# A ninth slot for the experts' weights, and 37 small loads moved from GpSimd to ScalarE and SyncE

## The reference, cut to what matters

```python
for i in range(DEPTH):                       # two layers
    u = x @ w_in                             # conv_w_in or moba_w_in
    y = concat([mix(u), memory_attention(q_mem, mem_k, mem_v)]) @ w_o[i]
    x = layer_norm(ALPHA * x + y, ln1_g[i], ln1_b[i])
    # router: 4 groups of 8 experts, top 2 in the best group
    for g in range(4):                       # 8 experts each
        h = silu(x @ w_gate[g]) * (x @ w_up[g])
        out += (h * combine) @ w_down[g]
    x = layer_norm(ALPHA * x + out, ln2_g[i], ln2_b[i])
```

## Time and profile before

| | us |
|---|---|
| median of three executions | 2206.97 |
| the profiled execution's own time | 2208.19 |
| its span, first to last instruction | 2206.3 |
| TensorE busy | 2084.1 (94%) |
| VectorE busy | 1128.3 (51%) |
| ScalarE busy | 773.3 (35%) |
| GpSimd busy | 62.8 (3%) |

### The profile page before, as it was taken

How to read it: one execution, slowest core, us unless ns; L and a number is a source line. 1 busy time by engine, 2 the same in 40 slices (tenths; PEclk the granted TensorE clock), 3 DMA queues, 4 the chain that set the end, 5 groups by cost and what they waited for, 6 DMA issues and landing times.

```text
span 2206.3 us, 29568 instructions
## 1 busy us (share of the span) xinstructions
PE 2084.1 (94%) x12352; PEld 1470.8 (67%) x12352; DVE 1128.3 (51%) x1967; ACT 773.3 (35%) x1468; POOL 62.8 (3%) x96
## 2 busy tenths in 40 slices
PE   8989999999979899999999799999999999999998
PEld 7974433333358644333344588999888889999887
DVE  5964332222256543222222667567674676667665
ACT  4751111011035411101110355644654465544552
POOL 3000000000000000000000000011000000010000
PEclk9999999999989999999999899999999999999999
DMA  8628999999974389999999653454554724554552
GB/s 270 217 91 359 429 427 427 427 427 427 425 298 177 131 358 427 427 427 428 427 427 425 233 196 101 148 180 161 191 175 169 246 78 140 173 191 163 191 187 80
DMA packets 130251, 600.25 MB, mean 272 GB/s; under 512 B 6029, under 2 KB 26641, under 8 KB 103745
## 3 DMA queue, kind: packets, MB, share of 16 engines
q1 hardware_dynamic: 125808, 590.37, 67.8%
q10 hardware_dynamic: 3072, 6.74, 0.8%
q0 software_dynamic: 1232, 1.19, 0.4%
HBM read 597.22 MB, written 1.05 MB: 271 GB/s over the span
## 4 chain that ended last, share of the span: by engine, by line
PE 76%; DMA 16%; DVE 5%; ACT 2%; issue 1%; SPq 0%; DVEq 0%; ACTq 0%
PE ps L1609 12%; DMA ring<-in_w_up 10%; PE ps L470 7%; PE ps L1653 7%; PE ps L456 6%; PE ps L457 6%; PE ps L458 6%; DMA rx<-in_w_up 5%; PE ps L469 3%; PE ps L498 2%; PE ps L499 2%; PE ps L500 2%; PE ps L583 2%; PE ps L978 2%; PE ps L1538 1%; PE ps L3042 1%
## 5 line engine op out<-in xcount | busy, mean ns | idle before, releaser
L432 DVE TENSOR_TENSOR CL<-ring,CH 128x1024 fp32r<-128x1024 f32 x284 | 333.6, 1214 | 198.3 <-ACT CH L427 196.9
L1609 PE MATMUL ps<-ring,ARM 128*64 128x512 f32 x1024 | 352.4, 606 | 25.6 <-DMA ring<-in_w_up 19.7
L1609 PE MATMUL ps<-rx,ARM 128*64 128x512 f32 x1024 | 352.8, 606 | 22.5 <-DMA rx<-in_w_up 13.5
L427 ACT ACTIVATE CH<-ring 128x1024 fp32r<-128x1024 f32 x284 | 283.5, 1046 | 127.2 <-PE ps L3044 57.3
L1627 DVE TENSOR_TENSOR ARM<-ARM,ps 128x512 f32<-128x512 f32 x32 | 22.0, 688 | 438.8 <-PE ps L1609 438.8
L470 PE MATMUL ps<-XTHL,CH 128*128 128x512 f32 x704 | 240.6, 396 | 0.0
L1609 PEld LDWEIGHTS ps<-ring,ARM 128*64 128x64 f32 x1024 | 112.9, 139 | 181.4 <-issue 143.3
L1609 PEld LDWEIGHTS ps<-rx,ARM 128*64 128x64 f32 x1024 | 114.4, 139 | 174.3 <-issue 135.8
L456 PE MATMUL ps<-XTHL,CH 128*128 128x256 f32 x752 | 219.5, 292 | 0.0
L458 PE MATMUL ps<-XTHL,CL 128*128 128x256 f32 x752 | 212.7, 283 | 0.0
L457 PE MATMUL ps<-XTHL,CH 128*128 128x256 f32 x752 | 212.6, 283 | 0.0
(11 more groups left out here) (441 smaller groups left out, 3954.0 us busy)
## 6 DMA issues: line engine op xcount, KB each, us to landing
rx<-in_w_gate SPq DMA_DIRECT2D x34, 2048.0 KB, 24.7
ring<-in_w_up SPq DMA_DIRECT2D x32, 2048.0 KB, 26.2
ring<-in_w_gate SPq DMA_DIRECT2D x30, 2048.0 KB, 25.6
ring<-in_w_down SPq DMA_DIRECT2D x30, 2048.0 KB, 26.6
ring<-in_w_ffn SPq DMA_DIRECT2D x30, 2048.0 KB, 8.1
rx<-in_w_up SPq DMA_DIRECT2D x28, 2048.0 KB, 27.1
rx<-in_w_down SPq DMA_DIRECT2D x26, 2048.0 KB, 27.1
ring<-in_w_in SPq DMA_DIRECT2D x14, 2048.0 KB, 8.6
```

Of the source, the lines that this page charges most:

```text
L427: a.e.activation(pc.hi[:, cs], pc.ap[:, cs], ACT.Copy).then_inc(act_done, a.put("hi", pc.k, q))
L432: v.e.tensor_tensor(pc.lo[:, cs], pc.ap[:, cs], pc.hi[:, cs].bitcast(F), ALU.subtract).then_inc(dve_done, v.put("lo", pc.k, q))
L1609: i = p.e.matmul(b[64 * x:64 * x + 64, :], m.XG[:, c, s0 + 64 * x:s0 + 64 * x + 64], us[x].ap[:, c, :], start=c == 0, stop=c == 7)
```

## The change

A ninth slot, `ninth`, is added, which like the ring slots lives through the program, but only the experts use it. It stands first in the turn, so that u0 goes into it, u1 into the first extra slot, u2 to u5 into ring slots and u6 to u8 into the other extra slots; from u9 on a load waits for the unit nine places before it. The room comes from the descriptor area that was kept for GpSimd's DMAs (`dynamic_dma_scratch_size=256`) and from 32 columns of the scratch tile SM. GpSimd issues no DMA any more. Of its 37 loads ScalarE issues 8 right behind CST, and 12 (router weights and biases, ln1 gains) after its wait for x and ahead of x's high halves; SyncE issues the 8 lambda loads ahead of list entry 5, the positions ahead of u6 of layer 0 (with a wait for VectorE's second lambda sum, since COS and the lambda vectors now share CS), and 8 loads for block 2 ahead of layer 1's last `w_o` load. The waits for the counts change with them.

```diff
-        cst_in, x_in, vec_in, route_in = (sem(x + "_in") for x in ("cst", "x", "vec", "route"))
+        cst_in, x_in, vec_in, route_in, late_in = (sem(x + "_in") for x in ("cst", "x", "vec", "route", "late"))
+        pos_in = sem("pos_in")
+        ninth = Slot(sb("ninth", UNIT)[:, :], sem("ninth_in"), sem("ninth_in2"))
-        SM = sb("SM", 384)
+        SM = sb("SM", 352)
+                wo_last = loads[-1][0]
-                slots = extra[:1] + ring[k:] + ring[:k] + extra[1:]
+                slots = [ninth] + extra[:1] + ring[k:] + ring[:k] + extra[1:]
+        VEC_IN, ROUTE_IN, LATE_IN, LAM_IN = 16 * 8, 16 * 12, 16 * 8, 16 * 8
         def a_first_loads():
             a.e.dma_start(CST[:, :], I["cst"]).then_inc(cst_in, 16)
+            for k, name in enumerate(("conv_dw_b", "conv_ln_g", "conv_ln_b")):
+                a.e.dma_start(VR[6 * k:6 * k + 6, :], ...).then_inc(vec_in, 16)
+            a.e.dma_start(VR[18:66, :], ...).then_inc(vec_in, 16)
+            a.e.dma_start(VR[66:68, :], I["diff_subln_2"]).then_inc(vec_in, 16)
+            for k, name in enumerate(("cmp_pos_k_2", "cmp_pos_v_2")):
+                a.e.dma_start(PR[32 * k:32 * k + 32, :], ...).then_inc(vec_in, 16)
+            a.e.dma_start(DWR[0:31, :], I["conv_dw_w"][0]).then_inc(vec_in, 16)
+        def a_route_loads():
+            for l in range(2):
+                wr = WR[:, 288 * l:288 * l + 288].rearrange("p (c n) -> p c n", c=8)
+                a.e.dma_start(wr[:, :, 0:4], major(I["w_rg"][l], 0, 4)).then_inc(route_in, 16)
+                a.e.dma_start(wr[:, :, 4:36], major(I["w_re"][l], 0, 32)).then_inc(route_in, 16)
+                a.e.dma_start(BR[:, 36 * l:36 * l + 4], ...).then_inc(route_in, 16)
+                a.e.dma_start(BR[:, 36 * l + 4:36 * l + 36], ...).then_inc(route_in, 16)
+                for k, name in enumerate(("ln1_g", "ln1_b")):
+                    a.e.dma_start(GF[:, l, k, :], ...).then_inc(route_in, 16)
         def y_first_loads(k):
...
+            if k == 5:
+                y_lam_loads()
+            if loads[k][0] is MOE[0][1][1][0][0]:
+                y.wait_ge(dve_done, v.at("lam", 1))
+                y.e.dma_start(COS.bitcast(I32), I["positions_2"][0].partition_broadcast(128)).then_inc(pos_in, 16)
+            if loads[k][0] is wo_last:
+                y_late_loads()
-        def g_first_loads():
...
-        def g_route_loads():
-            g.wait_ge(x_in, 16)
...
+        def y_lam_loads():
+            for l in range(2):
+                for k, name in enumerate(("diff_lq1_2", "diff_lk1_2", "diff_lq2_2", "diff_lk2_2")):
+                    n = 256 * l + 64 * k
+                    y.e.dma_start(CS[:, n:n + 64], I[name][l].partition_broadcast(128)).then_inc(lam_in, 16)
+        def y_late_loads():
+            for l in range(2):
+                for k, name in enumerate(("attn_norm_2", "ffn_norm_2")):
+                    y.e.dma_start(GN[:, l, k, :], ...).then_inc(late_in, 16)
+                for k, name in enumerate(("cmp_k_w2_2", "cmp_v_w2_2")):
+                    y.e.dma_start(W2[:, n:n + 128]..., ...).then_inc(late_in, 16)
             a_transposed("mem", ms)
             a_next("mix0", 0)
+            a.wait_ge(x_in, 16)
+            a_route_loads()
             a_transposed("x0", MIX[0][1])
-        def pool_angles():
...
         def dve_lam(l):
-            lv = SIN.rearrange("p (k q d) -> p k q d", k=2, q=2)
-            v.wait_ge(lam_in, 16 * (9 if l else 4))
+            lv = CS[:, 256 * l:256 * l + 256].rearrange("p (k q d) -> p k q d", k=2, q=2)
+            v.wait_ge(lam_in, LAM_IN)
         def dve_angles():
-            v.wait_ge(lam_in, 16 * 9)
+            v.wait_ge(pos_in, 16)
         def act_begin():
+            a.wait_ge(late_in, LATE_IN)
         def pool_all():
-            g_first_loads()
             pool_memory()
-            g_route_loads()
-            pool_angles()
-    nc = bacc.Bacc("TRN2", target_bir_lowering=False, num_devices=1)
+    nc = bacc.Bacc("TRN2", target_bir_lowering=False, num_devices=1, dynamic_dma_scratch_size=256)
```

More of the change, by code:

```diff
@@ L228, in small @@
                 k = sum(m for _, m in places.values())
-                assert k + n <= 384, "SM is full"
+                assert k + n <= 352, "SM is full"
                 places[name] = (k, n)
@@ L758, in load_gb @@
             a.e.dma_start(GB[:, 1, :], bias.partition_broadcast(128)).then_inc(gb_in, 16)
+        VEC_IN, ROUTE_IN, LATE_IN, LAM_IN = 16 * 8, 16 * 12, 16 * 8, 16 * 8
         def a_first_loads():
             a.e.dma_start(CST[:, :], I["cst"]).then_inc(cst_in, 16)
+            for k, name in enumerate(("conv_dw_b", "conv_ln_g", "conv_ln_b")):
+                a.e.dma_start(VR[6 * k:6 * k + 6, :], I[name].rearrange("a (j p) -> (a j) p", p=128)).then_inc(vec_in, 16)
+            a.e.dma_start(VR[18:66, :], I["b_merge_2"].rearrange("l (j p) -> (l j) p", p=128)).then_inc(vec_in, 16)
+            a.e.dma_start(VR[66:68, :], I["diff_subln_2"]).then_inc(vec_in, 16)
+            for k, name in enumerate(("cmp_pos_k_2", "cmp_pos_v_2")):
+                a.e.dma_start(PR[32 * k:32 * k + 32, :],
+                              I[name].rearrange("l (j i) d -> (l j) (i d)", i=2)).then_inc(vec_in, 16)
+            a.e.dma_start(DWR[0:31, :], I["conv_dw_w"][0]).then_inc(vec_in, 16)
[4 more added lines that the diff above has]
+                a.e.dma_start(wr[:, :, 4:36], major(I["w_re"][l], 0, 32)).then_inc(route_in, 16)
+                a.e.dma_start(BR[:, 36 * l:36 * l + 4], I["b_rg"][l].partition_broadcast(128)).then_inc(route_in, 16)
+                a.e.dma_start(BR[:, 36 * l + 4:36 * l + 36],
+                              I["b_re"][l].partition_broadcast(128)).then_inc(route_in, 16)
+                for k, name in enumerate(("ln1_g", "ln1_b")):
+                    a.e.dma_start(GF[:, l, k, :], I[name][l].rearrange("(p c) -> p c", c=8)).then_inc(route_in, 16)
         def y_first_loads(k):
@@ L768, in y_first_loads @@
                 y.e.dma_start(X, I["x"][0].rearrange("(t p) d -> p t d", p=128)).then_inc(x_in, 16)
-        VEC_IN = 16 * 8
-        ROUTE_IN = 16 * 20
-        def g_first_loads():
[L774 to L781, removed]
@@ L783, in g_route_loads @@
-        def g_route_loads():
-            g.wait_ge(x_in, 16)
-            for l in range(2):
[L786 to L793, removed]
+            if k == 5:
+                y_lam_loads()
@@ L794, in g_route_loads @@
+        def y_late_loads():
+            for l in range(2):
                 for k, name in enumerate(("attn_norm_2", "ffn_norm_2")):
-                    g.e.dma_start(GN[:, l, k, :], I[name][l].rearrange("(p c) -> p c", c=8)).then_inc(route_in, 16)
+                    y.e.dma_start(GN[:, l, k, :], I[name][l].rearrange("(p c) -> p c", c=8)).then_inc(late_in, 16)
                 for k, name in enumerate(("cmp_k_w2_2", "cmp_v_w2_2")):
                     n = 256 * l + 128 * k
-                    g.e.dma_start(W2[:, n:n + 128].rearrange("p (c d) -> p c d", c=2),
-                                  I[name][l].rearrange("(c p) d -> p c d", p=128)).then_inc(route_in, 16)
+                    y.e.dma_start(W2[:, n:n + 128].rearrange("p (c d) -> p c d", c=2),
+                                  I[name][l].rearrange("(c p) d -> p c d", p=128)).then_inc(late_in, 16)
```

## The result

| | before | after |
|---|---|---|
| median, 12 executions each | 2206.14 us | 2210.33 us |
| lowest to highest | 2202.91 to 2208.34 | 2206.50 to 2212.29 |
| profiled execution, its span | 2208.19, 2206.3 | 2209.25, 2207.4 |

The changed kernel is slower: ratio 1.0020, 95% interval 1.0012 to 1.0027. The forecast was 2205, that is 1.9 us less than before; the medians put 4.2 us on it. 2210.33 lies within the stated range of 2194 to 2213, on the other side of the kernel before than the forecast. One execution of a later experiment (conv_dw_w in two loads) came out at 2335.1 us in a slow state, and its interval leaves it out.

A forecast was written before the change was run, and what follows sets the result against it. The prediction took DMA transfers to be the limit in the two experts' stages. The slot's -11.9 and the start's +10.0, all else 0, made -1.9 us: 2206.3 by the profile, 2205 as a median, range 2194 to 2213.

The forecast's parts named there:

- the likeliest case: At the start, many small pieces hold ScalarE's issues; with the slot's gain 2205 us, own range 2200 to 2210, chance 0.40.
- the third rival: At the start, ScalarE is not held but the route loads land 5 us late for VectorE; 2200 us, chance 0.15.
- the second: Rival at the start: ScalarE is not held and all loads pass freely; 2195 us, chance 0.28.
- the fifth: Rival in the experts' stages: the ninth slot brings nothing, what follows waits on the ring; 2217 us, chance 0.03.
- I take 10.0: Loss at the start in us: 8.0 from x's high halves coming late on ScalarE, 2 from TensorE's low clock.
- the 25 quick turns: At the start, by the skill's rule: 320 small pieces drain in some 25 turns, ScalarE through by about 24 us.
- Together 11.9: Ninth slot's gain in both layers' experts' stages, in us; bounds 9.8 and 14.8.
- the price of one place in the stream: In the experts' loads, one unit's place further on: 4.9 us, the lower bound of a layer's gain.
- The 5.1 for layer 0: Ninth slot's gain in us in layer 0's experts, taken between 4.9 and 7.4.
- The 6.8 for layer 1: Ninth slot's gain in us in layer 1's experts, whose stop is a single gap just ahead of a landing.
- the band of no change: Whole kernel: times a measurement cannot tell from no change, about 0.2%, 4.4 us; bounds 2202.6 and 2211.4.
- The fourth rival: Ahead of x, one DMA engine carries DWR's 31 rows, x lands 3.9 us later; 2211 to 2213 us, chance 0.14.

The follow-up runs named there:

- conv_dw_w in two loads: The changed kernel with the load of conv_dw_w's 31 rows cut into 16 and 15 rows; 2210.35 us.
- routes on SyncE: The changed kernel with the router's twelve loads issued by SyncE at about 54 us and VectorE's router work moved later; 2195.45 us.
- nine in layer 1: The kernel of routes on SyncE with eight slots in layer 0 and nine in layer 1; 2201.15 us.

## Why the prediction was wrong

**What held.** ScalarE is held, through the pieces of its own queue, as the likeliest case had it; the ninth slot lets every release free a unit one place further on, and the gain is all in the experts' stages; nothing comes of the lambda loads, and nothing shows of the late and position loads, which weren't moved by themselves; loads behind the experts aren't late, as the earlier trace rows let expect. VectorE's router work runs at 51.91 and waits for no DMA, so the third rival is out, as are the second (issues stay short) and the fifth.

**What failed: "I take 10.0".** The loss is 12.8 us by medians (12.2 beside the same chip's kernel before). Its first term is mis-sized: ScalarE was to be released at 33.5 and was at 36.0. One part is x's landing, 1.4 later. One is the start: the first small piece moved at 21.6, 4.2 us behind the first issue, where I had 2 and 18.5. The third is the limit. I took 160 packets an engine from SyncE's convolution loads, between bounds of 142 and none. The queues over 17 to 24.8, when the issue of 6.03 us ends:

```profile
q1 hardware_dynamic: 1458, 2.81, 101.5%
q10 hardware_dynamic: 530, 0.03, 5.6%
```

The first three loads have (1024 + 1024 + 128) / 16 = 136 pieces an engine, and 530 / 16 = 33 had gone: 103 left, not 160, and below my lower bound. The next three long issues (ends at 26.30, 32.39 and 34.52) leave 95, 64 and 68 by the same count. In the changed kernel the issues of SyncE's second and third convolution loads (ends at 12.31 and 17.74) leave (2816 - 660) / 16 = 135 and (3840 - 1932) / 16 = 119. In routes on SyncE its two long issues leave (3200 - 1051) / 16 = 134 at 60.87 and (3328 - 3160) / 16 = 10 at 66.85. So no fixed number of outstanding pieces ends a hold, and what does stays open.

I let 160 pieces an engine go before ScalarE was free; by 35.5 it had been 243. In return the pieces went faster than I had them. Over 17 to 35.5, then over 22 to 28 and 28 to 31:

```profile
q1 hardware_dynamic: 4181, 5.40, 92.5%
q10 hardware_dynamic: 3889, 0.24, 16.3%
...
q1 hardware_dynamic: 1030, 2.08, 97.0%
q10 hardware_dynamic: 1029, 0.02, 12.0%
...
q1 hardware_dynamic: 990, 0.51, 76.0%
q10 hardware_dynamic: 2290, 0.16, 59.0%
```

3889 / 16 = 243 pieces an engine went in 18.5 us, 0.076 us each on the mean. Beside 2 KB pieces, over 22 to 28, a pair took 6 x 16 / 1029 = 0.093 us, where I had 0.11; beside SyncE's 256-byte pieces, over 28 to 31, a small one took 3 x 16 / 2290 = 0.021, where I had 0.05. The 1 : 1 of the two queues holds for small pieces beside 2 KB ones (1030 and 1029), but not over 28 to 31, where q10 moved 2.3 pieces for one of q1. The stretch of 1 : 1 doesn't decide between my reading and the Trainium skill's rule that I set against it ("DMA: Bandwidth & Descriptors", "Queues, rings and completion order"): several pieces of each queue in turn give the same ratio. What falls is my use of that rule, the 25 quick turns; its consequence, ScalarE through at about 24, didn't come.

What follows on 14.1 us of delay was in proportion: 12.2 at the first release, 0.87 of it, where I had 10.0 for 11.5.

**What failed: "Together 11.9".** The slot gives 8.6 (on the changed kernel) to 9.8 (on routes on SyncE). In the stages it is 4.8 and 4.5, or 5.3 and 4.7: the price of one place in the stream, 4.9, which I had as the lower bound. The 5.1 for layer 0 was right. The 6.8 for layer 1 was not: I added a stop of the stream, and no gain for it is in the stages. Layer 1's profile before, at 441.33, seemed to bear out the 6.8 and was 2.2 to 2.6 us off layer 1 in the other profiles with eight slots. Such a stage can take 441 by itself: nine in layer 1 shows 441.25 in its layer 0, which has eight.

One reading counts for nothing in the sum but was wrong: slice 15 stood at 358 GB/s, so the full slices of layer 1 are 16 to 22.

**The sum.** 12.8 lost and 8.6 won are 4.2 slower, where -11.9 + 10.0 gave 1.9 faster. Each term was off by 2 to 3 us in the direction that flattered the change. Between two terms of ten, a sum of 2 carried no sign; a likeliest case inside the band of no change was the most that could be said, with slower nearer than I had it. The fourth rival's mechanism was there at 1.5 instead of 3.9 us, on its own too little. That the range held the time is in part luck: its upper end, 2213, was that rival's price, and the likeliest case's own range ended at 2210.

## What to carry to other kernels

Ahead of an engine's work that others wait for, count the pieces of the loads it issues, not their bytes or their number: with 320 small pieces an engine ScalarE's twelve issues took 18.7 us, with 96 for the same bytes in the same place 5.7, none of them held. Either load the matrix as it stands in memory and pick it apart on chip, or let a queue issue it that has a pause. And a gain that is the difference of two terms of its own size needs each measured alone, best by undoing one.

## What the runs showed of the hardware

- A DMA issue can take 6 us (6.03 and 6.37 on ScalarE, 6.08 and 5.94 on SyncE, against 0.45): the engine that issues stands still, and with it everything behind it in its order. This came with many pieces issued ahead. It did not end at a fixed number of them: between 10 and 166 for each of the 16 DMA engines were left when a long issue ended.
- A small piece (16 to 128 bytes) took 0.012 us on an engine with nothing large in turn with it (70 to 71 in routes on SyncE), and 0.093 us where a 2 KB piece went for each of them (22 to 28 in the changed kernel).
- TensorE's granted clock over one stretch of a stage came out at 1.00, 0.77 or 0.66 in kernels that do the same there, and in executions of one kernel too, for 4 to 7 us (0.2 to 0.3%) of the whole (163.0 and 164.2 against 168.0 to 169.9). What picks the level stays open: the moment at which the stage starts doesn't (last landings at 618.0 and 618.4 gave 0.77, 617.7 and 619.0 gave 1.00, 618.7 gave 0.66). A comparison of kernels under 0.3% needs many executions of each, and the stage times from the profiles beside them.
